# High and low halves of x side by side in an FFN's gate/up matmuls, with a filter network moved to the first chunk, on one Trainium2 core

## What is computed

```python
def swiglu_ffn(x, w_gate, w_up, w_down):
    return (jax.nn.silu(x @ w_gate) * (x @ w_up)) @ w_down

def hybrid_layer(x, ...):
    x = x + 0.5 * swiglu_ffn(rms_norm(x, ffn1_norm), ffn1_w_gate, ffn1_w_up, ffn1_w_down)
    proj = rms_norm(x, mix_norm) @ w_in
    ...
    x = x + jnp.concatenate([y_hy, y_mla, y_gla], axis=-1) @ w_out
    x = x + 0.5 * swiglu_ffn(rms_norm(x, ffn2_norm), ffn2_w_gate, ffn2_w_up, ffn2_w_down)
```

## Time and profile before

| | us |
|---|---|
| median of 3 runs | 1041.32 (1041.07 to 1041.56) |
| the profiled execution's own time | 1041.18 |
| its span | 1039.2 |
| PE busy in the span | 1011.4 |
| DVE busy, ACT busy, POOL busy | 643.8, 491.4, 117.0 |

### The profile page before, as it was taken

The page is one execution under the profiler, slowest core; times in us unless marked ns, Lnnn a source line. Parts: engine busy times, 40 slices in busy tenths (PEclk is TensorE's granted clock), DMA queues, the critical chain, the costliest instruction groups (busy, mean ns, idle before and its releaser), DMA issues.

```text
span 1039.2 us, 17426 instructions
## 1 busy us (share of the span) xinstructions
PE 1011.4 (97%) x7004; PEld 923.5 (89%) x7004; DVE 643.8 (62%) x738; ACT 491.4 (47%) x663; POOL 117.0 (11%) x160
## 2 busy tenths in 40 slices
PE   7999999999899999999999999999998999999997
PEld 6999999888778999999999999997886889999996
DVE  4655555676986655555566555557689765555555
ACT  6444434357754544343354443434576555434342
POOL 2000000150531200000020000003315220000001
PEclk9999999999999999999999999999999999999999
DMA  9565555343403554555555545552542236455541
GB/s 304 187 230 203 167 197 180 143 162 133 152 18 146 198 205 168 197 177 186 182 179 202 202 167 196 180 184 84 201 147 97 81 145 220 166 198 177 186 182 41
DMA packets 27084, 175.93 MB, mean 169 GB/s; under 512 B 3200, under 2 KB 3712, under 8 KB 6560
## 3 DMA queue, kind: packets, MB, share of 16 engines
q1 hardware_dynamic: 25744, 172.90, 46.4%
q0 software_dynamic: 720, 1.95, 0.7%
q10 hardware_dynamic: 576, 0.45, 0.1%
HBM read 174.58 MB, written 1.05 MB: 169 GB/s over the span
## 4 chain that ended last, share of the span: by engine, by line
issue 50%; PE 38%; POOL 9%; DVE 1%; DMA 1%; POOLq 1%; ACT 0%; SPq 0%; DVEq 0%; ACTq 0%
PE psum L1030 13%; PE psum L1031 13%; PE psum L1032 13%; POOL mixer_scratch L344 4%; POOL mixer_scratch L365 1%; POOL mixer_scratch L364 1%; DMA x<-in_x_dram 1%; POOL statistics L317 1%; POOL statistics L315 1%; POOL statistics L328 0%; POOL x_normed L369 0%; DVE x L721 0%; POOL statistics L331 0%; POOLq L226 0%; POOL mixer_scratch L366 0%
## 5 line engine op out<-in xcount | busy, mean ns | idle before, releaser
L675 DVE TENSOR_TENSOR w_low<-w_raw,w_high 128x2048 fp32r<-128x2048 f32 x160 | 369.0, 2310 | 197.6 <-ACT w_high L403 197.5
L1030 PE MATMUL psum<-xT_high,w_high 128*128 128x256 f32 x1536 | 437.7, 285 | 1.9 <-DVE xT_low L685 1.6
L1031 PE MATMUL psum<-xT_low,w_high 128*128 128x256 f32 x1536 | 435.2, 283 | 0.0
L1032 PE MATMUL psum<-xT_high,w_low 128*128 128x256 f32 x1536 | 435.1, 283 | 0.0
L403 ACT ACTIVATE w_high<-w_raw 128x2048 fp32r<-128x2048 f32 x160 | 304.9, 1910 | 95.3 <-PE psum L1032 92.3
L1030 PEld LDWEIGHTS psum<-xT_high,w_high 128*128 128x128 f32 x1536 | 295.1, 192 | 6.1 <-issue 4.4
L1031 PEld LDWEIGHTS psum<-xT_low,w_high 128*128 128x128 f32 x1536 | 295.3, 192 | 2.0 <-issue 0.5
L1032 PEld LDWEIGHTS psum<-xT_high,w_low 128*128 128x128 f32 x1536 | 295.2, 192 | 0.0
L451 ACT ACTIVATE silu_gate<-hidden 128x256 f32<-128x256 f32 x88 | 36.8, 418 | 299.1 <-DVE hidden L700 299.1
L1030 PE MATMUL psum<-w_high,hT_high 128*128 128x512 f32 (+1 forms) x360 | 140.0, 389 | 0.1
L1031 PE MATMUL psum<-w_low,hT_high 128*128 128x512 f32 (+1 forms) x360 | 139.7, 388 | 0.0
(11 more groups left out here) (180 smaller groups left out, 793.5 us busy)
## 6 DMA issues: line engine op xcount, KB each, us to landing
w_raw<-in_w_dram SPq DMA_DIRECT2D x160, 1024.0 KB, 4.8
w_raw<-in_w_dram SPq DMA_DIRECT2D x8, 256.0 KB, 8.0
x<-in_x_dram SPq DMA_DIRECT2D x2, 512.0 KB, 5.8
mixer_scratch<-in_fil_dram POOLq DMA_DIRECT2D x2, 512.0 KB, 6.6
out_dram<-x_normed SPq DMA_DIRECT2D x3, 256.0 KB, 2.1
mixer_scratch<-in_fil_dram POOLq DMA_DIRECT2D x2, 352.0 KB, 6.1
mixer_scratch<-in_fin_dram SPq DMA_DIRECT2D x1, 512.0 KB, 5.4
dft<-in_dft_dram SPq DMA_DIRECT2D x1, 256.0 KB, 5.1
```

Of the source, the lines that this page charges most:

```text
L675: e.tensor_tensor(WL[p][:], raw[p][:], WH[p][:].bitcast(F32), ALU.subtract).then_inc(s_lo.sem, 1)
L1030: e.matmul(out, ah, bh, start=start, stop=False)
L1031: e.matmul(out, ah, bl, start=False, stop=False)
L1032: return e.matmul(out, al, bh, start=False, stop=stop)
```

## The change

1. **gate/up.** High and low x lie side by side in one tile (`XB`), so that the high weight tile is held once while 512 columns stream (high x, then low x); the low weight tile follows with 256 columns (`split_passes`). Three passes become two, with as many columns. Gate and up of a half have a bank each (4 + 2*half + g), with the low x part in columns 256 to 511. ACT copies that part of both banks to SBUF (`part_copy`, 128 x 512), DVE adds the other one to it (`add_parts`, 128 x 512), and gate_normed and gate read the sum from SBUF. All chunks use the same four banks, so gate_up(c,h) waits for the `add_parts` of chunk c-1, half h.
2. **Filter network.** Both stages are in the first chunk, in bank 3. The first `argument` moves behind `ht_low` of half 0 and its `sine` behind `ht_high`, ahead of the new `part_copy` and `add_parts` of half 1; the second `filter_mm` is ahead of down(0), the second `argument` and `sine` ahead of all of chunk 2 on DVE and ACT. The second gate_up of chunk 1 no longer waits for `argument`, the fourth group of down(0) waits until the second one has read bank 3.
3. **Padded slots.** Three mixer slots are half or a quarter full; `hi` and `lo` treat the used columns alone (`filled`).
4. **Start.** The second half of x is fetched ahead of the first weight quarter; DVE doesn't wait for x any more (PE and ACT wait for its halves themselves). POOL fetches the filter's data after the second group of transposed x, in place of after x.

```diff
@@ -107,4 +107,4 @@
         xn = sb("x_normed", [P, T, D])
-        XH = sb("xT_high", [P, KD, SEQ], F32R)
-        XL = sb("xT_low", [P, KD, SEQ], F32R)
+        XB = sb("xT_split", [P, KD, 2, SEQ], F32R)
+        XH, XL = XB[:, :, 0, :], XB[:, :, 1, :]
         sg = sb("silu_gate", [P, 2, SEQ])
@@ -165,2 +165,3 @@
         assert cols[0] <= 16896, cols[0]
+        part, both = NV[:, 0], NV[:, 1]
...
@@ -244,2 +247,8 @@
+        def filled(v, n):
+
+            if not isinstance(n, int):
+                return v[:]
+            return v[:, 0:2, 0:256] if n == S_UQR else v[:, 0:2, :] if n in (S_UQN, S_UKV) else v[:]
+
         def halves(v):
@@ -279,5 +288,4 @@
             half_x(0, s_in0)
-            part(0, 0)
             half_x(1, s_in1)
-            for n, q in ((0, 1), (0, 2), (0, 3), (1, 0), (1, 1), (1, 2), (1, 3)):
+            for n, q in ((0, 0), (0, 1), (0, 2), (0, 3), (1, 0), (1, 1), (1, 2), (1, 3)):
                 part(n, q)
@@ -351,3 +359,3 @@
-                e.wait_ge(s_x.sem, s_x.at(l, 4))
+                e.wait_ge(s_xh.sem, s_xh.at(l, 2))
                 for rows_, a, b in ((HYF, F_Z, F_SKIP), (P, F_WIN, F_Z), (1, F_SKIP, NFIL)):
@@ -402,3 +410,3 @@
                 e.wait_ge(s_used.sem, l * SLOTS + n + 1)
-                e.activation(WH[p][:], raw[p][:], ACT.Copy).then_inc(s_hi.sem, 1)
+                e.activation(filled(WH[p], n), filled(raw[p], n), ACT.Copy).then_inc(s_hi.sem, 1)
...
@@ -448,2 +459,6 @@
+            def part_copy(l, q, f, slot):
+                e.wait_ge(s_used.sem, used(l, slot))
+                e.activation(part, PS[:, 4 + 2 * f:6 + 2 * f, SEQ:2 * SEQ], ACT.Copy).then_inc(s_part.sem, 1)
+
             def silu(l, q, f):
@@ -464,3 +479,5 @@
                 turned(l, j, turn, col, base)
-                hi(l, base + 2); hi(l, base + 3)
+                hi(l, base + 2)
+                part_copy(l, f * CH, 0, base)
+                hi(l, base + 3)
                 rstd_row(l, f)
@@ -472,2 +489,4 @@
                     for h in range(2):
+                        if c is not first or h:
+                            part_copy(l, q, h, base + h if c is first else base + 3 * c - 4 + h)
                         silu(l, q, h)
@@ -476,2 +495,4 @@
                         ht_high(l, q, h, 1 - pr)
+                        if f == 0 and c is first and h == 0:
+                            sine(l, 0, H1)
                     hi(l, base + 3 * c + 1, (pos(base + 1), base // RING + c + 1))
@@ -480,3 +501,3 @@
                 if f == 0:
-                    sine(l, 0, H1)
+                    sine(l, 1, H2)
                 with e.Fori(0, (CH - 3) // 2) as i:
@@ -486,2 +507,3 @@
                 q, pr = f * CH + CH - 1, (CH - 1) % 2
+                part_copy(l, q, 0, base + FFN_SLOTS - 4)
                 silu(l, q, 0)
@@ -489,6 +511,5 @@
                 ht_high(l, q, 0, pr)
+                part_copy(l, q, 1, base + FFN_SLOTS - 3)
                 silu(l, q, 1)
                 ht_high(l, q, 1, pr)
-                if f == 0:
-                    sine(l, 1, H2)
@@ -674,3 +695,3 @@
                 e.wait_ge(s_hi.sem, s_hi.at(l, n + 1))
-                e.tensor_tensor(WL[p][:], raw[p][:], WH[p][:].bitcast(F32), ALU.subtract).then_inc(s_lo.sem, 1)
+                e.tensor_tensor(filled(WL[p], n), filled(raw[p], n), filled(WH[p], n).bitcast(F32), ALU.subtract).then_inc(s_lo.sem, 1)
@@ -697,5 +718,9 @@
-            def gate_normed(l, q, f, pr, slot):
-                e.wait_ge(s_used.sem, used(l, slot))
-                e.tensor_tensor(hid[:, f, :], PS[:, 4 + 2 * pr + f, 0:SEQ], row, ALU.mult).then_inc(s_gn.sem, 1)
+            def add_parts(l, q, f):
+                e.wait_ge(s_part.sem, s_part.at(l, 2 * q + f + 1))
+                e.tensor_tensor(both, PS[:, 4 + 2 * f:6 + 2 * f, 0:SEQ], part, ALU.add).then_inc(s_both.sem, 1)
+
+            def gate_normed(l, q, f):
+                e.wait_ge(s_both.sem, s_both.at(l, 2 * q + f + 1))
+                e.tensor_tensor(hid[:, f, :], both[:, 0, :], row, ALU.mult).then_inc(s_gn.sem, 1)
@@ -703,3 +728,3 @@
                 e.wait_ge(s_silu.sem, s_silu.at(l, 2 * q + f + 1))
-                e.scalar_tensor_tensor(out=hid[:, f, :], in0=PS[:, 4 + 2 * pr + f, SEQ:2 * SEQ], scalar=0.5 * float(D) ** 0.5, in1=sg[:, f, :],
+                e.scalar_tensor_tensor(out=hid[:, f, :], in0=both[:, 1, :], scalar=0.5 * float(D) ** 0.5, in1=sg[:, f, :],
                                        op0=ALU.mult, op1=ALU.mult).then_inc(s_h.sem, 1)
@@ -732,3 +757,4 @@
                 a, t = ARG[0:HYF], TURN[0:HYF]
-                link(l, e.tensor_scalar(a, PS[0:HYF, bank, 0:SEQ], par[0:HYF, b:b + 1], par[0:HYF, f:f + 1], ALU.add, ALU.mult))
+                e.tensor_scalar(a, PS[0:HYF, bank, 0:SEQ], par[0:HYF, b:b + 1], par[0:HYF, f:f + 1], ALU.add, ALU.mult).then_inc(f_rd.sem, 1)
+                e.wait_ge(f_rd.sem, f_rd.at(l, n + 1))
                 link(l, e.tensor_scalar(t, a, 1 / (2 * math.pi), ROUND, ALU.mult, ALU.add))
@@ -749,3 +775,5 @@
                     lo(l, base + 1)
-                lo(l, base + 2); lo(l, base + 3)
+                lo(l, base + 2)
+                add_parts(l, f * CH, 0)
+                lo(l, base + 3)
@@ -754,3 +782,5 @@
                     for h in range(2):
-                        gate_normed(l, q, h, 1 - pr, base + h if c is first else base + 3 * c - 4 + h)
+                        if c is not first or h:
+                            add_parts(l, q, h)
+                        gate_normed(l, q, h)
                         gate(l, q, h, 1 - pr)
@@ -759,8 +789,10 @@
                         ht_low(l, q, h, 1 - pr)
+                        if f == 0 and c is first and h == 0:
+                            argument(l, 0, 3, C_FB1, C_FF1)
                     lo(l, base + 3 * c + 1, pos(base + 1))
                 first = 1
-                if f == 0:
-                    argument(l, 0, 7, C_FB1, C_FF1)
                 e.wait_ge(s_rc.sem, s_rc.at(l, f + 1))
                 chunk(first, 1)
+                if f == 0:
+                    argument(l, 1, 3, C_FB2, C_FF2)
                 with e.Fori(0, (CH - 3) // 2) as i:
@@ -770,3 +802,4 @@
                 q, pr = f * CH + CH - 1, (CH - 1) % 2
-                gate_normed(l, q, 0, pr, base + FFN_SLOTS - 4)
+                add_parts(l, q, 0)
+                gate_normed(l, q, 0)
                 gate(l, q, 0, pr)
@@ -774,3 +807,4 @@
                 ht_low(l, q, 0, pr)
-                gate_normed(l, q, 1, pr, base + FFN_SLOTS - 3)
+                add_parts(l, q, 1)
+                gate_normed(l, q, 1)
                 gate(l, q, 1, pr)
@@ -778,3 +812,2 @@
                 if f == 0:
-                    argument(l, 1, 7, C_FB2, C_FF2)
                     lo(l, S_G3)
@@ -876,7 +909,3 @@
             e.memset(KR[0:DR, 1, :], 0.0).then_inc(s_kz.sem, 1)
-            e.wait_ge(s_in0.sem, 16)
-            e.sem_inc(s_x.sem, 2)
-            e.wait_ge(s_in1.sem, 16)
-            e.sem_inc(s_x.sem, 2)
-            e.wait_ge(s_cst.sem, 16)
+            e.sem_inc(s_x.sem, 4)
             for l in range(DEPTH):
@@ -1033,2 +1062,7 @@
+            def split_passes(out, ah, al, k):
+
+                e.matmul(out, ah, XB[:, k, :, :], start=k == 0, stop=False)
+                return e.matmul(out[:, 0:SEQ], al, XH[:, k, :], start=False, stop=k == KD - 1)
+
             def turn_group(l, j, g, bank, tiles):
...
@@ -1108,2 +1145,4 @@
                         e.wait_ge(s_hl.sem, s_hl.at(l, 2 * q + h + 1))
+                    if f == 0 and first and h == 0 and t * m:
+                        e.wait_ge(f_rd.sem, f_rd.at(l, 2))
                     r = passes(PS[:, t * 2 + m, :], HHB[pr][:, h, t * P:(t + 1) * P], HLB[pr][:, h, t * P:(t + 1) * P],
@@ -1126,4 +1165,3 @@
                         a = slice((k % 2) * 256 + g * P, (k % 2) * 256 + (g + 1) * P)
-                        r = passes(PS[:, 4 + 2 * pr + half, g * SEQ:(g + 1) * SEQ], WH[p][:, k // 2, a], WL[p][:, k // 2, a],
-                                   XH[:, k, :], XL[:, k, :], k == 0, k == KD - 1)
+                        r = split_passes(PS[:, 4 + 2 * half + g, :], WH[p][:, k // 2, a], WL[p][:, k // 2, a], k)
                 r.then_inc(s_used.sem, 1)
@@ -1153,9 +1191,9 @@
                     q = f * CH + (c - 1)
+                    e.wait_ge(s_both.sem, s_both.at(l, 2 * q + 1))
                     gate_up(l, turn, base + 3 * c - 1, pos(base + 2), 0, pr, False)
-                    if f == 0 and first:
-                        e.wait_ge(f_arg.sem, f_arg.at(l, 1))
+                    e.wait_ge(s_both.sem, s_both.at(l, 2 * q + 2))
                     gate_up(l, turn, base + 3 * c, pos(base), 1, pr, False)
-                    if f == 0 and c is last:
-                        filter_mm(l, 1, F_W2, H1, HYF, 7)
+                    if f == 0 and first:
+                        filter_mm(l, 1, F_W2, H1, HYF, 3)
                     down(l, base + 3 * c + 1, pos(base + 1), q, 1 - pr, first, False, f)
@@ -1163,3 +1201,3 @@
```

(24 more changed lines are left out.)

## The result

The changed kernel takes **1046.22 us** (median) against 1041.32: ratio 1.0043, 95% interval 1.0033 to 1.0054, **slower by 0.43%**. The forecast was 1034.7 with a range up to 1041.5, so both the sign and the range are missed. Two runs of this document were in a slower state of the chip and are left out of the ratios: one of the six of the changed kernel, at 1113.77 us, and one of the four of the variant with the filter network in three places, at 1411.88. The profiled execution is 1045.72, its span 1043.7 against 1039.2.

The account below looks back on a forecast made before the run. PE was taken to bound the kernel, busy 1011.4 of 1039.2 us. The sum was 1041.2 - 18.2 (passes) + 13.5 (waits) - 1.8 (padded slots) = 1034.7 us, range 1025.5 to 1041.5.

Parts of the forecast that it names:

- Gate/up passes: All four FFNs: 1408 steps go from 0.360 to 0.347 us, 13 ns less each, 18.2 us saved.
- the sign turns: Gate/up step of 0.352 us, above which the forecast had the change become slower instead of faster.
- Waits: PE waits at FFN 1's first chunks, ahead of gate_up(1,1), gate_up(2,0) and behind: 7.5 in layer 0, 5.95 in layer 1; +13.5 us.
- The two 0.55 behind gate_up(2,0): Further PE wait of 0.55 us for the lo of base+6 in FFN 1, once in each layer.
- Clock: Rival, 22%: clock falls behind FFN 1's waits, each costing 2.1 us more less 0.55 covered; 1038, or 1042 at worst.
- Padded slots: Mixers: less DVE and ACT work shortens PE's waits by 0.9 us a layer, -1.8 in all.
- What leaves the last chunk was hidden by PE's passes there, so nothing comes back: Last chunk of FFN 1: moving filter work out of it gains no time, 0 us.
- Start: Kernel start: PE may begin some tenths earlier, but in layer 0 only waits longer at gate_up(1,1); 0 us.
- The dear alternation: Rival, 12%: gate/up 512 passes beside 256 passes keep 0.236, a 0.356 step; gain only 5.6 us, time 1047.3.

Follow-up runs that it names:

- the variant with the filter network in three places: Changed kernel with the filter network taken apart again, out of the crowded first chunk, at three places in FFN 1: 1032.42 us, ratio 0.9913.
- the experiment with the filter alone: Kernel before with only the filter network moved into the first chunk, old passes, weights and start kept: 1044.37 us, ratio 1.0043.
- the five variants with waits in the first chunk: Changed kernel with grouped passes, second argument's rest late, half 1 first, or whole slots; kernel before with the filter move alone: 1041.27 to 1045.64 us.
- the grouped one: Changed kernel with each gate or up product's eight 512-column passes first, then its eight 256-column passes: 1042.73 us, ratio 1.0015.
- the one with half 1 first: Changed kernel with half 1's part_copy and add_parts ahead of the first sine and argument: 1042.91 us, ratio 1.0019.
- the one with whole slots: Changed kernel with filled undone, so ACT and DVE split the padded slots whole again: 1045.64 us, ratio 1.0047.
- The best two: Changed kernel with filter network in three places and grouped passes, 1030.54 us; the same with x's second half behind the first weight quarter, 1028.95 us.

## Why the prediction was wrong

- **Gate/up passes: -18.2, measured -9.1.** This is the step that failed. A step was taken at the steady 0.227 + 0.120 = 0.347 and takes 0.353, 0.236 + 0.117, in 145 of 176 products. Its grounds, "since every step stands in a long run of like steps", did not hold: a step has two changes of width, and the rows at such changes (0.24 for the first long pass behind short ones, 0.22 and 0.11 at the other change) gave bounds that were nearer than the steady rows. They did not give the answer either, since the passes do go at 0.347 in some stretches of the same kernel. The 0.353 lies just past the point where the forecast said the sign turns, 0.352; with the other terms as forecast it gives 1043.8. The rule of the Trainium skill ("TensorE: Matmul & The Clock Gate", "Back-to-back issue gap", N/2.4 + 2.5 ns, there the gap of an isolated matmul) had 325 ns for a step and 3.5 us for the whole gain. Neither fits: the pass intervals of 236 and 229 to 230 ns for 512 columns are above its 215.8, and the gain is 2.6 times its.
- **Waits: +13.5, measured +12.2.** Right in place, releaser and size. The forecast had 2.65, 4.3, 1.1 and 4.3 and got 2.47, 4.34, 1.02 and 4.36. It had half 1 added at 33.7, and PE started at 33.6. Without the 0.7 of ordinary spacing they are 11.5. The two 0.55 behind gate_up(2,0) did not appear. They rested on PE running at full speed behind the wait, and it did not; no run tests that by itself.
- **Clock: 0, measured about +4.5.** It stood as a rival with 22%, priced at 2.1 less 0.55 for each wait; a stretch measured 1.5, and there were three. The rival's time, 1038 to 1042, kept the 18.2 for the passes; with 9.1 it would have been 1047 to 1051.
- **Padded slots: -1.8, measured -1.0.** Inside its bounds of 0 to 5.7 a layer, but taken as 0.9 a layer where 0.5 is right.
- **"What leaves the last chunk was hidden by PE's passes there, so nothing comes back"**: wrong by 1.4. PE's passes there hid it, but the work behind it on DVE (and on ACT: `sine`, `hi` and `lo` of S_G3, updates of x, `diag_rstd`) came later for it, and PE waited for that some 4 us on, outside the FFN. The rows that show it are in the trace of the kernel before (its stop of 0.46 us and the chain ahead of it, in the experiment with the filter alone).
- **Start: 0**, measured -0.35 in the profile.

With the measured terms: 1041.2 - 9.1 + 12.2 + 4.5 - 1.0 - 1.4 - 0.35 = 1046.0, the profiled execution being 1045.7 (with 11.5 for the waits it is 1045.3). The dear alternation, with 12%, was right in the size of a step, and only in part in the reason. It left the passes a gain of 5.6 where they had 9.1, and had no clock in it, so that its 1047.3 came close for a wrong reason: the two errors nearly cancel. The error in the chances was to treat alternation and clock as exclusive; together they were no remote case.

## What to carry to other kernels

Where a change makes PE alternate between two widths, cost each pass from rows at a change of width as well as from steady rows, take the two as bounds, find the step at which the sign turns, and try the passes grouped. But grouping asks for all operands of the first group early. When work is moved off a place because it was hidden there, and onto a place where PE's next operand is made, price both ends on the slower engine's queue: here 13.5 us of waits were foreseen and stood against a gain that was half as large, and keeping the filter network apart turns a 0.43% loss into a 0.87% gain. A PE wait of four microseconds should be charged with low clock as the expected case, not as a rival.

## What the runs showed of the hardware

- **Widths.** Intervals from a pass to the next, at full clock, split fp32r: 120 ns in runs of 256 columns and 227 in downs of 512; 117 and 236 when they alternate; 119 and 230 when grouped in eights. Neither DVE's nor ACT's activity moved them: with both idle throughout, the long one still took 236.4 (18 of them between 80 and 180 us of the changed kernel). When they alternate, the same passes go either at 0.353 or at 0.347 a step (0.230 + 0.117), and keep the pace until the order is broken. What decides between the two stays open.
- **The clock behind waits.** Over the changed kernel and the five variants with waits in the first chunk: behind all eight waits of 4.1 to 4.4 us (two each in the changed kernel, the grouped one, the one with half 1 first and the one with whole slots) the clock was at 1.2 GHz for 3.4 or 6.8 us. In four (changed kernel, whole slots) it fell 0.8 to 1.3 us after PE had started again, in the other four 0.5 to 2.0 us before, while PE still waited. Of six waits of 1.9 to 2.6 us one was followed by a fall (2.47, changed kernel), five were not (1.90, 1.90, 2.58, 2.61, 2.61). Behind those of about 1.0 none was. The length of the wait alone does not decide in the middle band, and no run here shows what does.
- **Spread.** The kernel before stays within 0.5 us over the six runs beside the changed kernel and within 1.2 over 26 others. The ones with waits of 2 us and more spread over 2 to 3 us in 4 to 10 runs (the changed kernel from 1044.66 to 1047.1). The best two, whose start differs, are within 0.5 in four runs each. Why is open.
